# Three feed-forward blocks on one core: Strassen's seven products for four of the 22 feature pairs of each up projection, and a later place for SiLU and the product

## What is computed

```python
D_MODEL, SEQ, D_FF, CONV_W = 1024, 512, 2816, 3

def conv_ffn(h, w_up, conv_w, conv_b, w_down):
    seq = h.shape[1]
    u = h @ w_up                                     # 512x1024 @ 1024x5632
    up = jnp.pad(u, ((0, 0), (CONV_W - 1, 0), (0, 0)))
    u = sum(up[:, j:j + seq] * conv_w[j] for j in range(CONV_W)) + conv_b
    a, b = u[..., :D_FF], u[..., D_FF:]
    return (jax.nn.silu(a) * b) @ w_down             # 512x2816 @ 2816x1024
```

## Time and profile before

| | us |
|---|---|
| median of 3 runs | 2128.41 (2128.15 to 2129.32) |
| the profiled execution's own time | 2127.71 |
| its span, first to last instruction | 2125.9 |
| TensorE busy | 2107.9 (99%) |
| VectorE, ScalarE, GpSimd busy | 1318.7, 1017.3, 907.7 |
| granted TensorE clock | 1.0 throughout |

### The profile page before, as it was taken

The page is one execution under the profiler, slowest core; times in us unless marked ns, Lnnn a source line. Parts: engine busy times, 40 slices in busy tenths (PEclk is TensorE's granted clock), DMA queues, the critical chain, the costliest instruction groups (busy, mean ns, idle before and its releaser), DMA issues.

```text
span 2125.9 us, 27915 instructions
## 1 busy us (share of the span) xinstructions
PE 2107.9 (99%) x10587; PEld 1779.9 (84%) x10587; DVE 1318.7 (62%) x2236; ACT 1017.3 (48%) x1570; POOL 907.7 (43%) x452
## 2 busy tenths in 40 slices
PE   9999999999999999999999999999999999999999
PEld 7868889889888888887898898888887888898888
DVE  7973676657634445475676574997577324685673
ACT  6564544444432424355444444445877434544442
POOL 3504444434534343433444434665433554434433
PEclk9999999999999999999999999999999999999999
DMA  4203233223322232222232324322222242323322
GB/s 166 70 11 103 90 100 101 99 89 105 119 84 90 84 99 75 93 77 90 89 110 99 99 82 175 106 82 80 70 68 70 92 140 80 109 95 104 100 87 92
DMA packets 57669, 200.59 MB, mean 94 GB/s; under 512 B 6400, under 2 KB 7168, under 8 KB 57280
## 3 DMA queue, kind: packets, MB, share of 16 engines
q1 hardware_dynamic: 56816, 197.46, 28.3%
q10 hardware_dynamic: 720, 1.34, 0.2%
HBM read 194.32 MB, written 4.19 MB: 93 GB/s over the span
## 4 chain that ended last, share of the span: by engine, by line
PE 90%; DVE 5%; ACT 2%; issue 1%; DMA 0%; POOL 0%; SPq 0%; ACTq 0%; DVEq 0%
PE ps L393 23%; PE ps L395 23%; PE ps L394 23%; PE ps L666 4%; PE ps L667 4%; PE ps L668 4%; PE ps L423 2%; PE ps L422 2%; PE ps L421 2%; ACT SC L765 1%; DVE SC L910 1%; PE ps L2229 1%; DVE SC L916 1%; PE ps L1622 1%; PE ps L2214 0%
## 5 line engine op out<-in xcount | busy, mean ns | idle before, releaser
L371 POOL TENSOR_TENSOR WL<-WS,WH 128x1024 fp32r<-128x1024 f32 (+1 forms) x312 | 738.1, 2368 | 956.2 <-ACT WH L361 956.0
L393 PE MATMUL ps<-H,WH 128*128 128x512 f32 (+2 forms) x1776 | 693.1, 390 | 2.4 <-POOL WL L371 1.1
L395 PE MATMUL ps<-H,WL 128*128 128x512 f32 (+2 forms) x1776 | 690.0, 388 | 0.0
L394 PE MATMUL ps<-H,WH 128*128 128x512 f32 (+2 forms) x1776 | 689.9, 388 | 0.0
L361 ACT ACTIVATE WH<-WS 128x1024 fp32r<-128x1024 f32 (+2 forms) x314 | 324.7, 1035 | 248.0 <-PE ps L395 164.4
L393 PEld LDWEIGHTS ps<-H,WH 128*128 128x128 f32 (+1 forms) x1776 | 333.1, 188 | 75.9 <-issue 4.8
L395 PEld LDWEIGHTS ps<-H,WL 128*128 128x128 f32 (+1 forms) x1776 | 332.9, 187 | 69.4
L394 PEld LDWEIGHTS ps<-H,WH 128*128 128x128 f32 (+1 forms) x1776 | 333.2, 188 | 66.0
L765 ACT ACTIVATE SC<-ps,FP 128x512 f32<-128x512 f32 x132 | 102.8, 779 | 213.6 <-DVE ps L905 212.9
L393 PE MATMUL ps<-G,WH 128*128 128x512 f32 x496 | 193.6, 390 | 2.0 <-DVE G L1948 1.4
L666 PE MATMUL ps<-G_long,WH 128*128 128x256 f32 x672 | 191.0, 284 | 2.6 <-DVE X L888 1.6
(11 more groups left out here) (297 smaller groups left out, 2991.2 us busy)
## 6 DMA issues: line engine op xcount, KB each, us to landing
WS<-in_w SPq DMA_DIRECT2D x337, 512.0 KB, 3.3
WS<-in_w SPq DMA_DIRECT2D x24, 384.0 KB, 3.0
xs<-X SPq DMA_DIRECT2D x1, 2048.0 KB, 6.3
X<-xs SPq DMA_DIRECT2D x8, 256.0 KB, 4.2
out<-X SPq DMA_DIRECT2D x8, 256.0 KB, 2.0
X<-in_sg SPq DMA_DIRECT2D x1, 1344.0 KB, 5.7
X<-in_x ACTq DMA_DIRECT2D x4, 256.0 KB, 6.0
X<-in_x SPq DMA_DIRECT2D x4, 256.0 KB, 5.5
```

The source lines that it names most:

```text
L371: e.tensor_tensor(lo, raw, hi.bitcast(F), ALU.subtract).then_inc(*P.sig("w_lo", i))
L393: e.matmul(out, lh, rh, start=start, stop=False)
L394: e.matmul(out, lh, rl, start=False, stop=False)
L395: return e.matmul(out, ll, rh, start=False, stop=stop)
```

## The change

1. **Four pairs by seven products.** Pairs 7, 12, 15 and 18 of each up projection (`UP_PAIRED`) are no longer two features of 24 matmuls with 512 tokens, but seven products of 12 matmuls with 256 tokens (`pe_up_pair`). The two features are the two rows of blocks, the even and odd blocks of the model's width the two columns, the two halves of the tokens the columns of the other factor. Four sums of weight blocks are made by GpSimd (`pool_up_pair`), and GpSimd makes all seven lo parts; ScalarE the seven hi parts.
2. **The turned input.** The sums and differences of the normed input that the products need (t1 to t4, for four pairs of blocks) are made once in each feed-forward part, during pairs 1 to 6: ScalarE scales x again (`scaled`, 2 operations of 512), GpSimd makes four sums of 256, ScalarE rounds 1024 columns (`turned_hi`), VectorE takes the rest (`turned_lo`), four times each.
3. **Copies between the products.** Three products and their sums build up in one half of a bank. ScalarE copies that half after the first and third product (p1, u2) and another half after the second (p5); VectorE adds p5 to the chain after the fifth (c22), and both copies to the other feature at the end (c11). TensorE waits for p1 before the third product, for p5 before the fourth, u2 before the fifth, c22 before the seventh.
4. **Order.** SiLU, `mul`, `product` and the forms of pair p now stand among the operations of pair p + 1, so that an engine does something of one pair while another works on the other. "Make hi as far as there" stands before `tap2` of the first feature, not after it. The convolution uses two buffers instead of four. Ahead of a group of down pairs, the sums s1, s2, s3 and their lo parts stand earlier in VectorE's program, and two PSUM banks swap their roles.

The loads, the arithmetic of other pairs and the down products stay.

The diff, cut to its core:

```diff
+def pe_up_pair(P, e, L, p):
+    pair = (L, p)
+    for z in range(2):
+        listed(P, ("ups", L, p, z))
+    a, b = bank(P, e, ("up", L, p)), bank(P, e, ("up", L, FT + p))
+    left, right, chain = a[:, 0:256], a[:, 256:512], b[:, 0:256]
+    def rows(k, half):
+        c = slice(256 * half, 256 * half + 256)
+        return [(P.H(2 * q + k, 0)[:, c], P.H(2 * q + k, 1)[:, c]) for q in range(4)]
+    def turned(name):
+        return [(f_tx(P, q, 0, name), f_tx(P, q, 1, name)) for q in range(4)]
+    pe_product(P, e, pair, "a11", "w_lo", chain, rows(0, 0), True)
+    e.wait_ge(*P.at("t_lo", (L, 3)))
+    pe_product(P, e, pair, "s1", "w_lo", right, turned("t1"), True)
+    e.wait_ge(*P.at("ct", (pair, "p1")))
+    pe_product(P, e, pair, "s2", "w_lo", chain, turned("t2"), False)
+    e.wait_ge(*P.at("ct", (pair, "p5")))
+    pe_product(P, e, pair, "a12", "w_lo", left, rows(1, 0), False)
+    e.wait_ge(*P.at("ct", (pair, "u2")))
+    pe_product(P, e, pair, "s3", "w_lo", chain, turned("t3"), False)
+    pe_product(P, e, pair, "s4", "w_lo", right, rows(1, 1), False)
+    e.wait_ge(*P.at("c22", pair))
+    pe_product(P, e, pair, "a22", "w_lo", chain, turned("t4"), False)
+    P.cell_n += 1
...
+    def part(pair, name, dst, src, ready):
+        e.wait_ge(*P.at("prod", (pair, ready)))
+        e.activation(dst, src, ACT.Copy).then_inc(*P.sig("ct", (pair, name)))
+    def scaled(q):
+        if q > 1:
+            e.wait_ge(*P.at("t_sum", (L, q - 2)))
+        for z in range(2):
+            k = 2 * q + z
+            e.activation(f_scaled(P, q)[:, z * T:z * T + T], P.X(k), ACT.Identity, scale=P.par(ph, k)).then_inc(
+                *P.sig("t_eo", (L, q, z)))
+    def turned_hi(q):
+        e.wait_ge(*P.at("t_sum", (L, q)))
+        e.activation(f_tx(P, q, 0), f_tx(P, q, 1, None, F), ACT.Copy).then_inc(*P.sig("t_hi", (L, q)))
+    def first_forms(p):
+        if p in UP_PAIRED:
+            act_form(P, e, (L, p), "a11")
+            act_form(P, e, (L, p), "s1", f_s1(P))
...
-            tap2(p, s)
+            if p > a:
+                silu(p - 1)
+                if paired:
+                    hi_to(P, e, P.ahead(("up", L, FT + p + 1)) - LEAD)
+                    product(p - 1)
+            if not paired and p < z - 1:
+                hi_to(P, e, P.ahead(("up", L, p), True))
+            tap2(p)
+            if ahead:
+                act_form(P, e, pair, "a12")
+            if p > a and not paired:
+                product(p - 1)
+            if paired:
+                hi_to(P, e, P.ahead(("up", L, FT + p + 1)) + 1 - LEAD)
+            if p == z - 1:
+                act_form(P, e, (L, g, 0), "s2")
+                act_form(P, e, (L, g, 0), "a12")
+                act_form(P, e, (L, g, 0), "s3")
+            if ahead:
+                act_form(P, e, pair, "s2", f_s1(P))
             forms_1(p - 1)
-            if p < z - 1:
-                hi_to(P, e, P.ahead(("up", L, p), True))
+            if p == z - 1:
+                forms_2(p - 1)
+                break
+            if ahead:
+                act_form(P, e, pair, "s3", P.raw(pair, "a21"))
+                part(pair, "p1", f_part(P)[:, 0:256], P.ps(("up", L, FT + p + 1))[:, 0:256], "a11")
+            tap2(FT + p)
+            if ahead:
+                act_form(P, e, pair, "a22")
+                part(pair, "p5", f_s5(P, p), P.ps(("up", L, p + 1))[:, 256:512], "s1")
+                act_form(P, e, pair, "s4", P.raw(pair, "a12"))
             forms_2(p - 1)
-            if p < z - 1:
-                tap2(FT + p, s + 1)
+            if ahead:
+                part(pair, "u2", f_part(P)[:, 256:512], P.ps(("up", L, FT + p + 1))[:, 0:256], "s2")
+                P.hi_n = P.index.get(("ups", L, p + 1, 1), 0) + 1
+            elif not paired:
                 hi_to(P, e, P.ahead(("up", L, FT + p), True))
-                silu(p)
-                product(p)
-        for name in ("s2", "a12", "s3", "s4", "a22"):
+            first_forms(p + 2)
+            if 2 <= p < 6:
+                turned_hi(p - 2)
+            if 1 <= p < 5:
+                scaled(p - 1)
...
+            if paired:
+                x, y = P.ps(("up", L, p)), P.ps(("up", L, FT + p))
+                mul(p - 1)
+                e.wait_ge(*P.at("prod", (pair, "s3")))
+                e.tensor_tensor(y[:, 256:512], y[:, 0:256], f_s5(P, p), ALU.add).then_inc(*P.sig("c22", pair))
+                forms_0(p - 1)
+                forms_1(p - 1)
+                e.wait_ge(*P.at("prod", (pair, "s4")))
+                e.tensor_tensor(x, x, f_part(P), ALU.add).then_inc(*P.sig("c11", pair))
             scale(p)
-            forms_1(p - 1)
-            tap1(p, s)
-            tap0(p, s)
+            if p > a and not paired:
+                mul(p - 1)
+            if p == z - 1:
+                dve_sum_lo(P, e, (L, g, 0), "s1")
+                dve_sum(P, e, (L, g, 0), "s3")
+                dve_sum(P, e, (L, g, 0), "s2")
+            tap1(p)
+            tap0(p)
+            if p > a and not paired:
+                forms_0(p - 1)
+                forms_1(p - 1)
+            elif p == a:
+                forms_1(p - 1)
+            if p == z - 1:
+                dve_sum_lo(P, e, (L, g, 0), "s2")
+                dve_take(P, e, (L, g, 0), "a11", "A", 0, 0)
+                dve_sum(P, e, (L, g, 0), "s4")
+                dve_sum_lo(P, e, (L, g, 0), "s3")
+            if p == z - 1:
+                break
+            scale(FT + p)
             forms_2(p - 1)
-            if p < z - 1:
-                scale(FT + p)
-                tap1(FT + p, s + 1)
-                tap0(FT + p, s + 1)
-                mul(p)
-                forms_0(p)
-        pair = (L, g, 0)
-        dve_sum(P, e, pair, "s3")
-        dve_sum(P, e, pair, "s2")
-        dve_sum_lo(P, e, pair, "s1")
-        dve_sum_lo(P, e, pair, "s2")
-        dve_sum(P, e, pair, "s4")
-        last, slot = z - 1, 2 * ((z - 1) % 2) + 1
+            tap1(FT + p)
+            tap0(FT + p)
+            forms_3(p - 1)
+            if 2 <= p < 6:
+                turned_lo(p - 2)
...
+def pool_up_pair(P, e, L, p):
+    pair = (L, p)
+    a11, a12, a21, a22 = (P.raw(pair, name) for name in ("a11", "a12", "a21", "a22"))
+    e.wait_ge(*P.at(*P.raw_in(pair, 0)))
+    e.wait_ge(*P.at(*P.raw_in(pair, 1)))
+    e.tensor_tensor(f_s1(P), a21, a22, ALU.add).then_inc(*P.sig("f_sum", (pair, "s1")))
+    e.tensor_tensor(a21, a11, a21, ALU.subtract).then_inc(*P.sig("f_sum", (pair, "s3")))
+    pool_lo(P, e, pair, "a11", a11)
+    pool_lo(P, e, pair, "s1", f_s1(P))
+    e.tensor_tensor(f_s1(P), f_s1(P), a11, ALU.subtract).then_inc(*P.sig("f_sum", (pair, "s2")))
+    pool_lo(P, e, pair, "a12", a12)
+    pool_lo(P, e, pair, "s2", f_s1(P))
+    e.tensor_tensor(a12, a12, f_s1(P), ALU.subtract).then_inc(*P.sig("f_sum", (pair, "s4")))
+    pool_lo(P, e, pair, "s3", a21)
+    pool_lo(P, e, pair, "s4", a12)
+    pool_lo(P, e, pair, "a22", a22)
+    P.lo_n = P.index.get(("ups", L, p, 1), 0) + 1
...
+def pool_turned(P, e, L, q):
+    even, odd = f_scaled(P, q)[:, 0:T], f_scaled(P, q)[:, T:2 * T]
+    t1, t2, t3, t4 = (f_tx(P, q, 1, name, F) for name in ("t1", "t2", "t3", "t4"))
+    e.wait_ge(*P.at("t_eo", (L, q, 1)))
+    e.tensor_tensor(t1, even[:, 256:512], even[:, 0:256], ALU.subtract).then_inc(*P.sig("t_part", (L, q, 1)))
+    e.tensor_tensor(t3, odd[:, 256:512], even[:, 256:512], ALU.subtract).then_inc(*P.sig("t_part", (L, q, 3)))
+    e.wait_ge(*P.at("t_part", (L, q, 1)))
+    e.tensor_tensor(t2, odd[:, 256:512], t1, ALU.subtract).then_inc(*P.sig("t_part", (L, q, 2)))
+    e.wait_ge(*P.at("t_part", (L, q, 2)))
+    e.tensor_tensor(t4, odd[:, 0:256], t2, ALU.subtract).then_inc(*P.sig("t_sum", (L, q)))
...
-        lo_to(P, e, P.ahead(("up", L, FT + z - 1)))
+        for p in range(a, z):
+            if p in UP_PAIRED:
+                pool_up_pair(P, e, L, p)
+                continue
+            lo_to(P, e, P.ahead(("up", L, p)) - LEAD)
+            if 3 <= p < 7:
+                pool_turned(P, e, L, p - 3)
+            lo_to(P, e, P.ahead(("up", L, FT + p)) - LEAD)
```

More of the change, by code:

```diff
@@ L315, in raw_ends @@
     key = P.order[i]
[L316 removed]
+    if key[0] not in ("dns", "ups"):
         return [("w_lo", i)]
[L318 removed]
+    pair, second = key[1:-1], key[-1]
+    if key[0] == "ups":
+        return [("w_lo", (pair, "a22" if second else "s3"))]
     return [("w_lo", (pair, "a22")), ("fs", (pair, "s4"))] if second else [("w_lo", (pair, "a11")), ("fs", (pair, "s2"))]
@@ L352, in hi_to @@
 def hi_to(P, e, n):
-    while P.hi_n < min(n, len(P.order)) and P.order[P.hi_n][0] != "dns":
+    while P.hi_n < min(n, len(P.order)) and P.order[P.hi_n][0] not in ("dns", "ups"):
         i = P.hi_n
@@ L364, in lo_to @@
 def lo_to(P, e, n):
-    while P.lo_n < min(n, len(P.order)) and P.order[P.lo_n][0] != "dns":
+    while P.lo_n < min(n, len(P.order)) and P.order[P.lo_n][0] not in ("dns", "ups"):
         i = P.lo_n
@@ L662, in pe_product @@
     e.wait_ge(*P.at(low, key))
-    for q in range(4):
```

(9 more changed lines are left out.)

134 lines of the change are left out of this document (89 added, 45 removed).

## The result

| | before | changed |
|---|---|---|
| median | 2128.28 (4 runs, 2127.94 to 2129.32) | 2116.06 (4 runs, 2116.0 to 2118.51) |
| ratio | | 0.9946, 95% interval 0.9934 to 0.9957 |
| the profiled execution's own time | 2127.71 | 2116.02 |
| its span | 2125.9 | 2114.2 |

The change is faster by 12.2 us, 0.5%; by the two profiled executions it is 11.69 us. The forecast was 14.8 less.

The account below looks back on a forecast made before the run. TensorE, busy 2107.9 of 2125.9 us, was taken to bound the kernel. The terms -9.6 - 2.5 - 3.9 + 1.2 = -14.8 us from 2128.41 gave 2113.6 us, range 2110.5 to 2121.5.

Parts of the forecast that it names:

- The seven products: Up projection: 7 x 12 matmuls of 256 tokens replace 48 of 512, 0.80 us a pair, 9.6 us saved in all.
- Rival 4: Matmuls of the changed pairs start closer together, 0.1133 us apart, 0.56 us a pair more saved: 2106.9 us; chance 0.02.
- The wait at the start: TensorE's waits at the start of each up projection, 0.85 us a part, all go: 2.5 us saved.
- The groups: TensorE's waits at the groups of down pairs, 1.62 us a part, go by 80%: 3.9 us saved.
- rival 2: Groups of down pairs give nothing back, as VectorE's sums fall on GpSimd's work and delay lo parts: 2117.5 us; chance 0.13.
- The pairs' stalls: TensorE waiting for other engines in the paired pairs: 0.1 us a pair, 1.2 us added, ends 0 and +7.2.
- The turned input: Making it in pairs 1 to 6 fits idle ScalarE and GpSimd time: costed at nothing, 2 us a part if uncovered.
- What VectorE loses behind a pair: VectorE's forms wait for `product` until 10.3 us, making `scale` 1.5 us late; its bank is not wanted for eight units.

Follow-up runs that it names:

- the order alone: The changed kernel with no paired pair and no turned input, the new order kept: 2125.75 us (10 runs), ratio 0.9988.

## Why the prediction was right, and where it was not

It was right in sign and in range, 2.5 us too low. Step by step:

- **The seven products, -9.6.** Right: 0.120 us a step in all twelve pairs, and 9.7 us when the pairs alone are taken away (9.1 by the steps, with what they cost at the groups). Rival 4, a shorter step, did not come, nor did the 14.2 us by the Trainium skill's N / 2.4 GHz plus 2.5 ns (TensorE: Matmul & The Clock Gate, "Wait — 56ns, not 53.3ns?"). A slip beside the sum: 0.80 of 10.88 us is 7.4%, so the shorter matmuls give back 5 of the 12.5%, not 6.
- **The wait at the start, -2.5.** Right in size: 0.85 us a part is gone. Of the two reasons given, the place of the rounding ahead of `tap2` is not needed.
- **The groups, -3.9.** The step that failed; the runs give +0.6 (0 from the order alone). In group 2 what the text said would come early came early, the first addition by 2.0 us as it said; in group 1, with more of the pairs' work now ahead of it, that was 0.7. But "s1 of the next down pair still stands ahead of an addition TensorE waits for" was named and priced at 20% of the old waits. It is one instruction of 1.47 us ahead of an addition whose bank is wanted at once, and a second behind it. The sum at the earlier trace rows took 1.81 us where 0.69 would do, so its doubled length was in the rows, and rival 2 named it; the sum did not price it ahead of the addition. Rival 2, that the groups give nothing back, is what happened there (2117.5; with no stall in the pairs, as below, 2116.3, and 2116.06 was measured). Its picture, sums falling on GpSimd's work, was right as well, but what they delay is an addition, not the lo parts.
- **The pairs' stalls, +1.2.** 0: no break in twelve pairs. The margins by the trace are 0.81 to 0.87 us for the copies and c22 (0.4 was the smallest on paper), and the smallest is the next unit's lo part with 0.51 (0.8 on paper). GpSimd's part was seen too well off, ScalarE's too badly. That the total came out 2.5 us too low and not further off is partly luck: 1.2 us were charged here that did not come, against 4.5 us credited at the groups that did not come, and the base was the median, 0.7 above the profiled execution.
- **The turned input, 0.** Nothing on the path. It takes 12 x 3.7 = 44 us of GpSimd; with the 114 that is 158, and 154 were measured. Three of the four sums of 256 tokens take 0.74 us, but the first takes 1.72 at the median, longer than the bound of 1.30. GpSimd's first sum, and VectorE's lo of the turned input beside it:

```profile
238.92 1.72 POOL L1241 TENSOR_TENSOR turned_whole<-GF 128x256 f32<-128x256 f32 x1
```
```profile
237.45 2.59 DVE L1118 TENSOR_TENSOR turned_cut<-turned_whole,turned_cut 128x1024 fp32r<-128x1024 f32 x1 [0.53 <-ACT turned_cut L902]
```
VectorE ends at 240.04, GpSimd 0.6 later: as if it could begin only when VectorE had ended.
- **What VectorE loses behind a pair** (`product` behind a rounding whose cell is free at 8.64) was described and costed at nothing, as there is time until the next pair. So it is at a spacing of three; at two it costs 13.0 us, more than all four pairs gain.
